# Head norms of one call together, lane steps cut into smaller ones, weight splits ahead of lane steps, and the meta products ahead of the odd weight piece

## What is computed

```python
for l in range(2):                                   # first block
    h = rmsnorm(x, norm_gain[l]) * (1 + scale) + shift      # shift, scale, gate from silu(c) @ w_mod[l]
    q_a, k_a, v_a, g_a, q_i, k_i, w_i, q_b, k_b, v_b, g_b = split(h @ w_in[l])
    q_a, k_a = rmsnorm(q_a by heads), rmsnorm(k_a)
    att = sparse_attention(q_a, k_a, v_a, ...)       # 64 keys by an index score, softmax
    ret = head_groupnorm(retention(rotary(q_b), rotary(k_b), v_b))
    x = x + gate * (concat(att * silu(g_a), ret * silu(g_b)) @ w_out[l])
proj = rms_norm(concat(meta_tokens, x)) @ w_in_2     # second block
sb = stick_breaking_attention(sb_q, sb_k, sb_v)
fox = forgetting_attention(rms_norm(fq by heads), rms_norm(fk by heads), fv, log_sigmoid(flogit + b))
x = x + concat(rms_norm(sb), rms_norm(fox) * sigmoid(fgate)) @ w_out_2
h = rms_norm(x)                                      # experts: 8 heads, 16 experts per head and token
q = h @ w_query; best experts of each token by product keys; a = gelu(<u_row, h>)
x = x + sum(g * a * v_row)
```

## Time and profile before

| | us |
|---|---|
| median of 3 runs (lowest, highest) | 3205.55 (3204.19, 3206.41) |
| the profiled execution's own time | 3203.59 |
| its span | 3201.7 |
| TensorE busy with matmuls | 2155.5 (67%) |
| VectorE busy | 1710.8 (53%) |
| ScalarE busy | 869.0 (27%) |
| mean granted TensorE clock | 0.838 of full speed |

### The profile page before, as it was taken

How to read it: one execution, slowest core, us unless ns; L and a number is a source line. 1 busy time by engine, 2 the same in 40 slices (tenths; PEclk the granted TensorE clock), 3 DMA queues, 4 the chain that set the end, 5 groups by cost and what they waited for, 6 DMA issues and landing times.

```text
span 3201.7 us, 30897 instructions
## 1 busy us (share of the span) xinstructions
PE 2155.5 (67%) x12338; PEld 1479.8 (46%) x12338; DVE 1710.8 (53%) x2746; ACT 869.0 (27%) x1327; POOL 794.7 (25%) x680
## 2 busy tenths in 40 slices
PE   5899999989998999999989981222323233222235
PEld 2676777877787777666668871000000000000001
DVE  3436556554656654343445689556555655565430
ACT  1333444444454444553535420000000000000000
POOL 1111100000000000000000025555555555555552
PEclk8999999999999999999989995666666666666667
DMA  9898864557754545343325687999999999999998
GB/s 385 286 299 282 280 198 148 184 177 246 220 170 137 165 143 162 106 138 99 118 76 170 212 311 304 421 421 422 421 421 422 421 421 422 422 420 422 422 422 339
DMA packets 243594, 901.01 MB, mean 281 GB/s; under 512 B 20374, under 2 KB 45228, under 8 KB 177004
## 3 DMA queue, kind: packets, MB, share of 16 engines
q0 software_dynamic: 94208, 612.85, 47.6%
q1 hardware_dynamic: 148768, 285.58, 27.6%
q10 hardware_dynamic: 476, 0.62, 0.1%
HBM read 894.78 MB, written 2.10 MB: 280 GB/s over the span
## 4 chain that ended last, share of the span: by engine, by line
PE 54%; DMA 30%; DVE 9%; ACT 3%; issue 2%; POOL 1%; SPq 0%; DVEq 0%; ACTq 0%; POOLq 0%
PE pp L1718 47%; DMA late<-in_peer_v,MI 10%; PE tp L1718 6%; DMA P<-in_peer_v,MI 5%; DMA ring<-in_peer_v,MI 5%; DMA x<-in_peer_v,MI 4%; DVE wL L1067 2%; DMA SY<-in_peer_v,MI 2%; PE tp L1721 2%; DMA late<-in_w_mod 2%; ACT wH L583 1%; DMA ring<-in_peer_w_query 1%; DMA ring<-in_w_in 1%; DMA SY<-in_w_mod 1%; DVE P L1677 0%
## 5 line engine op out<-in xcount | busy, mean ns | idle before, releaser
L1067 DVE TENSOR_TENSOR wL<-ring,wH 128x1024 fp32r<-128x1024 f32 (+3 forms) x504 | 582.2, 1161 | 598.3 <-ACT wH L583 594.9
L1718 PE MATMUL pp<-wH,hH 128*128 128x512 f32 (+3 forms) x1888 | 749.0, 397 | 38.9 <-DVE wL L1067 28.5
L1718 PE MATMUL pp<-wH,hL 128*128 128x512 f32 (+3 forms) x1888 | 717.5, 380 | 0.0
L1718 PE MATMUL pp<-wL,hH 128*128 128x512 f32 (+3 forms) x1888 | 717.1, 380 | 0.0
L583 ACT ACTIVATE wH<-ring 128x1024 fp32r<-128x1024 f32 (+3 forms) x504 | 505.4, 1008 | 473.3 <-PE pp L1718 316.5
L1718 PEld LDWEIGHTS pp<-wH,hH 128*128 128x128 f32 x1888 | 359.2, 190 | 182.5 <-issue 71.0
L1718 PE MATMUL pp<-late,S 128*32 128x512 f32 x736 | 227.3, 874 | 296.0 <-DMA P<-in_peer_v,MI 75.7
L1718 PEld LDWEIGHTS pp<-wH,hL 128*128 128x128 f32 x1888 | 358.4, 190 | 63.8
L1718 PEld LDWEIGHTS pp<-wL,hH 128*128 128x128 f32 x1888 | 359.8, 191 | 55.8 <-issue 1.2
L1718 PE MATMUL pp<-P,S 128*32 128x512 f32 x376 | 269.6, 885 | 151.6 <-DMA x<-in_peer_v,MI 75.8
L1718 PE MATMUL pp<-x,S 128*32 128x512 f32 x376 | 166.5, 880 | 223.1 <-DMA ring<-in_peer_v,MI 223.1
(11 more groups left out here) (302 smaller groups left out, 3005.7 us busy)
## 6 DMA issues: line engine op xcount, KB each, us to landing
ring<-in_w_in SPq DMA_DIRECT2D x288, 512.0 KB, 4.4
ring<-in_w_out SPq DMA_DIRECT2D x96, 512.0 KB, 4.4
P<-in_w_mod POOLq DMA_DIRECT2D x85, 512.0 KB, 5.0
late<-in_w_mod SPq DMA_DIRECT2D x64, 512.0 KB, 9.1
SY<-in_w_mod POOLq DMA_DIRECT2D x43, 512.0 KB, 5.3
ring<-in_w_in SPq DMA_DIRECT2D x48, 368.0 KB, 4.2
ring<-in_peer_w_query SPq DMA_DIRECT2D x32, 512.0 KB, 5.0
ring<-in_w_in SPq DMA_DIRECT2D x24, 344.0 KB, 3.2
```

The lines of the kernel that those rows point to most:

```text
L1067: tt(lo, raw, hi.bitcast(F32), ALU.subtract).then_inc(*tick("dve_lo", *names))
L1718: return e.matmul(o, l, r, start=start, stop=stop, skip_group_check=skip)
```

## The change

1. `norm_heads` takes the place of `head_rms`. All slices of a call are squared in one step, DVE runs one `rstd` chain over all their columns in the next, and one step later ACT scales the first slice and DVE multiplies the others by a broadcast of the roots. In all there are 11 chains where there were 28.
2. Lane steps are divided: a `yield` more between logits and Exp in `sparse` and `fox_pair`; Abs, Exp and Ln of `stick` in three steps, its masks in one; `forget` takes its three groups of rows together, function by function; the sum of squares of the stick output goes from DVE to ACT, both slices at once.
3. `order()`: the splits of the piece three ahead are now issued right behind a piece, in front of the lane steps; `meta` stands in front of the odd piece; `meta_norm` is three parts at pieces 2, 4 and 6; `norm 4` and `norm 6` stand beside a later piece of p4 and p6; the second and fourth `fox_turn` open beside piece 3; the rates in p4 go from 0.8, 0.6 to 0.85, 0.9 (1.1, 1.1 from group 12).

```diff
@@ order()
             yield from beside(n, pc)
-            yield "piece", p, q
             if p == 4 and meta_part(c0, w):
                 yield "meta", p, q
+            yield "piece", p, q
+            if (p, q + 1) in place:
+                yield from splits(p, q + 1)
...
-            if l and n == 1:
-                yield "meta_norm",
-            if l and n == 2:
+
+        def beside_out(n, pc):
+            if l and n == 1 and pc in (2, 4, 6):
+                yield "meta_norm", pc // 2 - 1
+            if l and n == 2 and pc == 1:
                 yield "meta_h",
...
-    yield "norm", 4
...
     def beside_in2(n, pc):
+        if n == 0 and pc == 3:
+            yield "norm", 4
         if n and pc == 3:
             yield "drain", "M"
+        if n in (6, 12) and pc == 3:
+            yield "open", "X", "fox_turn", n // 12, FK
...
-    yield from project(4, after_in2, lambda n: (0.8 if n < 13 else 1, 0.6, 1), early_out2, beside_in2)
+    yield from project(4, after_in2, lambda n: (0.85 if n < 12 else 1.1, 0.9 if n < 12 else 1.1, 1), early_out2, beside_in2)
...
-    yield "norm", 6
+    yield "late_loads",
     for q, (g, c0, w, pc) in enumerate(PIECES[6]):
         yield from splits(6, q)
+        if q == 3:
+            yield "norm", 6
@@ scalar(): norm_heads
+            def norm_heads(R, parts, *name):
+                o = 0
+                for i, (v, nh, p) in enumerate(parts):
+                    act(R.S[0:p, o * 128:(o + nh) * 128], v, ACT.Square).then_inc(*tick(R.act, ("head squares", *name, i)))
+                    o += nh
+                yield
+                yield
+                v, nh, p = parts[0]
+                w.wait_ge(*at("head roots", *name))
+                for h in range(nh):
+                    hv = v[:, h * 128:(h + 1) * 128]
+                    act(hv, hv, ACT.Copy, scale=R.root[0:p, h:h + 1]).then_inc(
...
@@ vector(): norm_heads
+            def norm_heads(R, parts, *name):
+                n = sum(nh for _, nh, _ in parts)
+                yield
+                o = 0
+                for i, (v, nh, p) in enumerate(parts):
+                    w.wait_ge(*at("head squares", *name, i))
+                    e.tensor_reduce(R.ss[0:p, o:o + nh], heads(R.S[0:p, o * 128:(o + nh) * 128], nh), AX, ALU.add).then_inc(
+                        *tick(R.dve))
+                    o += nh
+                rstd(R.dve, R.root[:, 0:n], R.ss[:, 0:n], 128, R.ss[:, 0:n], R.rest[:, 0:n], ("head roots", *name))
+                yield
+                w.wait_ge(*now(R.dve))
+                o = parts[0][1]
+                for i, (v, nh, p) in enumerate(parts[1:], 1):
+                    hv = heads(v, nh)
+                    tt(hv, hv, R.root[0:p, o:o + nh].unsqueeze(2).to_broadcast([p, nh, 128]), ALU.mult).then_inc(
...
```

More of the change, by code:

```diff
@@ L871, in stick @@
                 if half:
-                    for _ in range(4):
-                        yield
+                    for t in range(2):
+                        w.wait_ge(*at("mixed heads", 3))
+                        act(SS[:, 0:1024], P[:, t, SQ:SQ + 1024], ACT.Square, accum_out=R.ss[:, t:t + 1]).then_inc(
+                            *tick(R.act, ("stick squares", t)))
+                        w.wait_ge(*now(R.act))
+                    yield
+                    yield
             def fox_pair(lane, g):
@@ L917, in fox_turn @@
                 n = {FQ: 4, FK: 5}[c0] + 6 * half
-                for t in range(2):
-                    w.wait_ge(*at("stored", 4, n, t))
-                    yield from head_rms(R, P[:, t, c0 + 512 * half:c0 + 512 * half + 512], 4, 128, (c0, half, t))
+                w.wait_ge(*at("stored", 4, n, 1))
+                if c0 == FK:
+                    w.wait_ge(*at("meta out", n))
+                yield from norm_heads(R, four_parts(c0 + 512 * half, half if c0 == FK else None), c0, half)
                 if c0 == FQ:
@@ L924, in fox_turn @@
                     return
-                w.wait_ge(*at("meta out", n))
-                yield from head_rms(R, PM[:, MFK + 512 * half:MFK + 512 * half + 512], 4, 16, (c0, half, 2))
                 yield from turn_keys(R, heads(R.H[:, 1024:2112], 4), (c0, half), scale=col("fox_k_gain_2"))
             def forget():
-                for t in range(3):
-                    p = 16 if t == 2 else 128
-                    e1 = q1[0:p, 0:8]
+                yield
+                places = [(lf[0:p, t, :], e1[0:p, :], t) for t, (p, e1) in enumerate(((128, q1), (128, q2), (16, q3)))]
+                for f, e1, t in places:
                     w.wait_ge(*at("forget in", t))
-                    act(e1, lf[0:p, t, :], ACT.Abs).then_inc(*tick("act_x", ("forget abs", t)))
-                    w.wait_ge(*now("act_x"))
+                    act(e1, f, ACT.Abs).then_inc(*tick("act_x"))
+                w.wait_ge(*now("act_x"))
+                for f, e1, t in places:
                     act(e1, e1, ACT.Exp, scale=-1.0).then_inc(*tick("act_x"))
-                    w.wait_ge(*now("act_x"))
+                w.wait_ge(*now("act_x"))
+                for f, e1, t in places:
                     act(e1, e1, ACT.Ln, bias=1.0).then_inc(*tick("act_x", ("forget ln", t)))
@@ L1332, in gate @@
                 R = ROOM[lane]
-                w.wait_ge(*at(*(("attended", l, 1, 1) if lane == "X" else ("head normed", "qb", l, half, 1))))
+                w.wait_ge(*at(*(("attended", l, 1, 1) if lane == "X" else ("head normed", "qb", l, half, 0))))
+                if lane == "Y":
+                    w.wait_ge(*at("head normed", "qb", l, half, 1))
                 w.wait_ge(*now("dve_stored"))
@@ L1484, in fox_turn @@
             def fox_turn(half, c0):
-                for t in range(2):
-                    yield from head_rms(RX, 4, 128, (c0, half, t))
+                yield from norm_heads(RX, four_parts(c0 + 512 * half, half if c0 == FK else None), c0, half)
                 if c0 == FQ:
@@ L2096, in src @@
                     return P[:, t, c + h * 128:c + (h + 1) * 128]
-                for _ in range(4):
+                for _ in range(3):
                     yield
+                w.wait_ge(*at("head normed", c0, half, 0))
                 if c0 == FQ:
```

138 lines of the change are left out of this document (73 added, 65 removed).

## The result

The changed kernel takes 3190.22 us (median of 6 runs, 3183.02 to 3193.05), the kernel before 3205.24 us in the same session. The ratio is 0.9947, with a 95% interval of 0.9936 to 0.9958: 15.0 us faster, where 49.4 were forecast. The median lies 0.2 us above the range's upper end.

A forecast was written before the change was run, and what follows sets the result against it. TensorE bounds the kernel ahead of p6, DMA the last stage at 416 GB/s. Removing 86.0 us, less 34.6 of new waits and 2 of clock, gives 49.4 us: 3154.2, forecast 3156 with 1.96 for the median; range 3128 to 3190.

The forecast's parts named there:

- What the change removes, 86.0 us: PE idle time removed in p0, p2, p3 and p4, 63.5 us; with the lower clock behind it, 86.0 us.
- What it adds, 34.6 us of new waits: Splits now precede lane steps, so DVE starts about 2.3 us behind a piece's end; PE's new waits sum to 34.6 us.
- the masks: In p4, PE waits four times for DVE's masks of `stick`: 1.8 us three times and 3.6 once, 9.0 us.
- the last Exp: In p4, rate 1.1 from group 12 puts `stick`'s last Exp into the step where PE wants it: 3.6 us.
- The diagonals of the gate rows: PE waits for DVE's gate work and diagonals: 3.4 and 1.2 us in p0, 1.2 in p2, sum 5.8 us.
- The twelve copies of forget rows: At (p4, 12, 7), copies one narrow piece ahead of PE, behind a split: 3.5 us, an estimate.
- the smaller ones: Estimated waits of 0.5 to 1.8 us for rotations, head norms, an Exp, mixes, meta sums and `fox_turn` queries: 12.7 us.
- Each would cost half of 4.64 us, 2.3 us: from 0 to 9, and I take 2.: Lower clock behind four new waits of 3.4 to 3.6 us: 2.3 us each, 0 to 9 in all, 2 taken.
- each wait of 2 us or more lowers the clock: Rival: about twelve new waits lower the clock, 28 us at 2.3 each; gain 23 us, 3182 us; chance 0.12.
- The slower rival, lagging lane steps: Rival: ACT's and DVE's lane steps late at each of 147 groups up to p5; at 0.6 us, 3244 us; chance 0.05.
- All covered: Rival: data and queues are ahead, only some 8 us of new waits come; gain 78 us, 3128 us; chance 0.15.
- Eaten behind p6: Rival: gathers wait for something not earlier, such as `peer_w_query` loads; within 6 us of before, about 3204; chance 0.03.

## Why the prediction was wrong

**What bounds the kernel:** right. PE ahead of p6, the DMA engines behind it. The last stage kept its length and its 416 GB/s, and an earlier start came out nearly in full at the end: p5's last group begins 15.7 us earlier (1769.8 against 1785.5), and the span is 14.4 shorter (3187.3 against 3201.7). PE's idle time in p0, p2, p3 and p4 came near what I had said: 15.9, 22.4, 0.4 and 23.8 us, where 11, 19, 0.5 and 25 were forecast. What did not come is p4's length, 509.5 us where 490 were forecast: the idle time went, and the time did not.

**What the change removes, 86.0 us:** nearly right in size, but by luck. Without the early splits the rest of the change took away 54.8 us of idle time (63.5 forecast) and 51.2 us at the lower level, which is 25.6 (22.5 forecast): 80.4 in the account, 75.7 in the medians. p3 is as forecast: 101 us long before, 92 after, with 5.8 us of idle time and 3.4 of the clock gone. But I had given all of it to the divided steps and the norms, and these gave 53.8 us by themselves: in p4, where I had all 39.9 us of idle time go, they leave 18.3. The other 21.9 us are the meta products', which I had put down as costing nothing and giving nothing of their own. They gave 19 us alone and 48 beside early splits. I looked at what they do for PE, where a piece's load is hidden, and not at the 38 splits that stood at the head of ACT's queue and waited 83.4 us for a load.

**What it adds, 34.6 us of new waits:** right in size, from the same pattern. The early splits added 33.1 us of idle time (65.6 against 32.5), and the step at the index keys began 2.4 us later, where I had 2.3 for every such step. Of the places that I had named, the masks came to 9.5 us (9.0 forecast, though one by one they were 3.9, 0.8, 2.0 and 2.8) and the last Exp to 4.0 (3.6). The diagonals of the gate rows came to 5.2 in all, where 5.8 were forecast on top of 2.0 that stay. The twelve copies of forget rows, 3.5 us, didn't come. I missed the index keys (3.8 and 3.6 us, 1.4 and 1.1 before) and the gate's store, which frees the bank (twice 2.7); they filled the place of the smaller ones, so the sum is better than its parts.

**The step that failed: "Each would cost half of 4.64 us, 2.3 us: from 0 to 9, and I take 2."** That is the clock behind the new waits. In the account above it cost 30.7 us: 61.4 us more at the lower level with early splits than without. It is wrong twice. I took for a bound a single row, the 3.20 us that left the clock at 1.00. That same wait of 3.20 us left it up in the run with the meta products alone too, so the row was no accident. But it is the exception, and waits of 2.0 and 2.8 us in the changed kernel lowered the clock. The trace of the kernel before had it already. Two stretches at the lower level stand there, the first just behind a wait of 1.97 us for `wL` that ended at 1591.1, the second behind the 3.2 us of the earlier trace rows, which ended at 676.9:

```profile
1592.60:1595.90 3.30, 3.30 (x11) 1.86 (x13) 1.89 (x2) 1.20 (x2) 0.00 (x0) 0.50 0.00 0
...
677.80:681.10 3.30, 3.30 (x13) 3.30 (x12) 2.25 (x4) 1.83 (x3) 0.00 (x0) 0.50 0.02 5
```

The first is one of the eight of the earlier trace rows, which I had all put behind 4.5 us and more. And I took one cost, that of the first stretch, for all: the masks' wait of 3.9 us had 13.7 us behind it, the one of 2.0 us had 10.2, and the eight of before were themselves between 3.3 and 17 us long.

The rival "each wait of 2 us or more lowers the clock" had the right mechanism, with 28 us for it and 3182 us; what it lacked to 3190 is the 5 to 10 us by which the removed part was too large. I gave it 0.12. What these runs show is on its side: waits of 2.0 and 2.8 us lowered the clock, and filling two waits with matmuls kept it at 1.00. The Trainium skill's section "HAM oscillation — how this bites in real kernels" (page "TensorE: Matmul & The Clock Gate") has the clock fall behind waits of some 3 to 5 us between bursts of matmuls. By that, the trace agrees for such waits, but for the 3.20 us; of shorter waits the section says nothing, and I had read it as a rule for any.

**The slower rival, lagging lane steps:** its mechanism was at work, but not strongly enough to make the changed kernel slower. The early splits cost 60.7 us here and 100 us on the undivided kernel, against the 37 that I had for them. The lag didn't come at all 147 groups: PE has 37 waits of over 0.4 us in the stretch of the account, 25 without early splits. **All covered** didn't happen. **Eaten behind p6** didn't either: the end came earlier by nearly all that p5 did.

**What the early split buys:** I called it the price of the change, and took it as what buys the waits for `wL`. In this kernel it bought nothing: with the splits behind, `wL` ends 1.7 us of waits in p2. The divided steps had already done that. It could have been guessed from the trace before, on ACT: the 5.28 us of the earlier trace rows were DVE's chain in one step, and once this is divided no split stands behind it.

What stays open is why one wait lowers the clock and another of its length doesn't, and how long it stays down.

## What to carry to other kernels

Where an engine serves both a stream that is filled ahead and a chain that another engine waits for, the chain's step goes first, and the stream's next buffer behind it; a buffer that is filled three pieces ahead can wait 2 us, PE cannot. Of several edits that attack the same wait, each should be run alone: here two of them together won 76 us, and a third, which was to help, took back four fifths of it. In a kernel like this one a wait of PE of 2 us or more is to be priced with the lower clock behind it, here at up to twice the wait's own length and more (5.1 us for 2.0), unless other engines set the pace there.

## What the runs showed of the hardware

- The clock falls behind much shorter waits than the 4.5 us that I had gone by. I counted all waits of PE of over 1.2 us between 110 and 1780 us in the traces of all fourteen kernels, and how many had a stretch at 1.2 GHz begin in them or up to 3 us behind: 2 of 94 of 1.2 to 2 us, 27 of 45 of 2 to 3 us, 33 of 42 of 3 to 4 us, 9 of 12 of 4 to 5 us, all 29 above. Of the twelve waits of over 3 us that are left, ten stood in a stretch that had begun before; the other two are the wait of 3.20 us in two kernels. Fifteen more stretches, up to 1680 us, began with no wait of over 1.2 us in the 3 us ahead of them, most of them behind one of 0.8 to 1.1 us; the longest was of 17.1 us. Most waits stand in several of the kernels, so these are not as many independent cases.
- The same wait can have a different stretch behind it: that for p0's index keys, 3.8 to 4.0 us in all five kernels with early splits, had 3.4 us at the lower level in the changed kernel and 6.8 in the other four. The last Exp of `stick`, 2.3 us in the kernel without early splits, had 3.4 us there and 10.2 in the two with filled waits, with the same instructions around it. Differences of this size may be what lies between executions of one kernel here (3183 to 3193, 3126 to 3137). The mean clock over the whole program, which every execution shows, goes in step with the time in the four of the kernel without early splits (0.841, 0.840, 0.839 and 0.837 at 3126.2, 3128.6, 3133.4 and 3136.7 us). In the six of the changed kernel it does not (0.839 at 3191.3 us, 0.837 at 3183.0).
- The lower clock costs nothing where PE is not the one that is waited for: 13.7 us of it at the start of p2 went away with the filled waits, and p1 and p2 kept their length to 0.1 us.
